# The down product of a feed-forward layer made by seven block products in place of eight

## The reference, cut to what matters

```python
def memory_cross_attention(h, mem_n, w_q, w_kv, w_o):
    q = (h @ w_q).reshape(B, T, XATTN_HEADS, XATTN_HEAD_DIM)
    ...
    p = jax.nn.softmax(s, axis=-1).astype(h.dtype)
    o = jnp.einsum('bhtm,bmhd->bthd', p, v).reshape(B, T, D_MODEL)
    return o @ w_o

def conv_glu_ffn(h, w_up, conv_w, conv_b, w_down):
    u = causal_dwconv(h @ w_up, conv_w) + conv_b
    a, b = jnp.split(u, 2, axis=-1)
    return (jax.nn.silu(a) * b) @ w_down          # [1024, 2816] @ [2816, 1024]

h = h + rmsnorm(y, g[5])                          # y is the layer's output
```

## Time and profile before

| what | value |
|---|---|
| median of 3 runs | 2668.46 us (2666.83 to 2671.12) |
| the profiled execution | 2670.99 us |
| its span | 2669.2 us |
| PE busy | 2591.1 us, 97% |
| DVE, ACT, POOL busy | 1659.6, 844.0, 1131.9 us |
| mean granted clock of TensorE | 0.992 |
| chain that ended last | PE 89%, DVE 4%, POOL 2%, ACT 2% |
| the down product's line (L2266) | 9% of that chain |

### The profile page before, as it was taken

How to read it: one execution, slowest core, us unless ns; L and a number is a source line. 1 busy time by engine, 2 the same in 40 slices (tenths; PEclk the granted TensorE clock), 3 DMA queues, 4 the chain that set the end, 5 groups by cost and what they waited for, 6 DMA issues and landing times.

```text
span 2669.2 us, 33144 instructions
## 1 busy us (share of the span) xinstructions
PE 2591.1 (97%) x13218; PEld 2174.4 (81%) x13218; DVE 1659.6 (62%) x2194; ACT 844.0 (32%) x1332; POOL 1131.9 (42%) x651
## 2 busy tenths in 40 slices
PE   6999899989999999999999999999999999999998
PEld 5788788877788777888888887888888888888887
DVE  4879978766512587666674558804555556476566
ACT  4011233334223433333332436212222222343342
POOL 2433100046632548777754444673223322242364
PEclk9999999999999999999999999999999999999999
DMA  4122333235312412222245553573333342466682
GB/s 153 56 94 97 99 124 127 95 104 206 112 62 79 158 58 86 79 87 79 87 149 191 169 178 121 186 258 106 134 111 111 130 147 94 159 251 211 223 315 111
DMA packets 147381, 360.25 MB, mean 135 GB/s; under 512 B 15173, under 2 KB 51229, under 8 KB 147100
## 3 DMA queue, kind: packets, MB, share of 16 engines
q1 hardware_dynamic: 65072, 177.81, 19.9%
q10 hardware_dynamic: 82156, 180.33, 18.9%
HBM read 268.90 MB, written 89.19 MB: 134 GB/s over the span
## 4 chain that ended last, share of the span: by engine, by line
PE 89%; DVE 4%; POOL 2%; ACT 2%; issue 1%; DMA 1%; ACTq 0%; POOLq 0%; DVEq 0%
PE pp L296 32%; PE pp L2213 13%; PE pp L494 11%; PE pp L2266 9%; PE pp L278 9%; PE pp L2953 2%; PE pp L1272 2%; POOL w_lo L3653 1%; PE pp L1944 1%; PE pp L1983 1%; POOL w_hi L3651 1%; DMA w_raw<-in_weights 1%; PE pp L1558 1%; PE pp L1597 1%; PE pp L444 1%
## 5 line engine op out<-in xcount | busy, mean ns | idle before, releaser
L3651 POOL CAST w_hi<-w_raw 128x1024 fp32r<-128x1024 f32 x184 | 222.2, 1207 | 990.3 <-PE pp L296 659.5
L296 PE MATMUL pp<-w_hi,act_hi 128*128 128x512 f32 x1344 | 535.9, 399 | 12.7 <-POOL w_lo L3653 9.9
L296 PE MATMUL pp<-w_lo,act_hi 128*128 128x512 f32 x1344 | 524.5, 390 | 0.0
L296 PE MATMUL pp<-w_hi,act_lo 128*128 128x512 f32 x1344 | 524.5, 390 | 0.0
L3653 POOL TENSOR_TENSOR w_lo<-w_raw,w_hi 128x1024 fp32r<-128x1024 f32 x184 | 468.9, 2549 | 14.7
L296 PEld LDWEIGHTS pp<-w_hi,act_hi 128*128 128x128 f32 x1344 | 253.0, 188 | 67.9 <-POOL w_lo L3653 10.8
L296 PEld LDWEIGHTS pp<-w_hi,act_lo 128*128 128x128 f32 x1344 | 252.6, 188 | 53.5
L296 PEld LDWEIGHTS pp<-w_lo,act_hi 128*128 128x128 f32 x1344 | 253.2, 188 | 48.3
L494 PE MATMUL pp<-act_hi,w_hi 128*128 128x512 f32 x480 | 192.7, 402 | 10.6 <-DVE act_lo L849 6.5
L2184 POOL TENSOR_TENSOR w_lo<-w_raw,w_hi 128x1024 fp32r<-128x1024 f32 x52 | 132.5, 2550 | 164.7 <-ACT w_hi L2178 164.6
L494 PE MATMUL pp<-act_lo,w_hi 128*128 128x512 f32 x480 | 190.5, 397 | 0.0
(11 more groups left out here) (468 smaller groups left out, 5282.9 us busy)
## 6 DMA issues: line engine op xcount, KB each, us to landing
w_raw<-in_weights SPq DMA_DIRECT2D x314, 512.0 KB, 3.5
z_s<-hg_st ACTq DMA_DIRECT2D x52, 512.0 KB, 4.1
hid_s<-ffn_cb ACTq DMA_DIRECT2D x22, 512.0 KB, 2.6
ffn_graw<-hid_s ACTq DMA_DIRECT2D x44, 256.0 KB, 3.1
hg_qkb<-hT_s SPq DMA_DIRECT2D x16, 512.0 KB, 8.1
qkvT_s<-mixin_o ACTq DMA_DIRECT2D x12, 512.0 KB, 2.8
gdn_qkv<-qkvT_s ACTq DMA_DIRECT2D x8, 768.0 KB, 6.4
front_x<-in_x ACTq DMA_DIRECT2D x8, 512.0 KB, 5.0
```

The costliest lines, as they stand in the source:

```text
L296: last = pe.matmul(dst, a[:, k, t * P:(t + 1) * P], columns(w, j, k, 0, n), start=(k == 0 and a is high and w is w_hi), stop=(k == NK - 1 ...
L3651: pool.tensor_copy(hi, raw).then_inc(w_split, 1)
```

## The change

**The down product.** The hidden activation (tokens by 2816) and the weights (2816 by 1024) are cut in two by two blocks: hidden rows are taken in pairs (even rows and odd rows; 11 pairs, `FG`), tokens in halves, output columns in halves. Seven block products (`DOWN`) take the place of eight. Each has 11 steps, a step being one 128x512 piece of activation (or of a sum) by one 128x512 piece of weights (or of a sum), for four tiles: 4 x 3 = 12 matmuls of 512 columns. So there are 77 steps and 77 x 12 = 924 matmuls.

**Sums of weights** (T1 to T4, `DownSums`): 11 groups of four blocks are loaded (1 MB each, three buffers), four subtractions of 128x512 are made on each group in place, and the group is stored. Groups 0 to 5 are loaded and stored by ACT's queue in Queries and subtracted by DVE there; groups 6 to 10 are loaded and stored by SP and subtracted by POOL, in its list after the fourth half of w_o's first strip, which is while attention runs. `softmax_of` for tiles 0 and 1 moves from Attention to Queries on DVE, in between.

**Sums of activations** (S1 to S4, `hidden_sums`): DVE makes four of 128x512 for each pair of finished hidden rows, ACT's queue stores them (1 MB), one pair in each two rounds of the up part, the first before `tlow(3)`.

**Weights of the down product.** From the third half on, SP loads the raw half to the place of its own low part, once PE has released that place; before, it went to `w_raw`. ACT makes the high part, DVE (POOL before) makes the low part in place (`split_half`). A half is two pieces, so two steps; the sixth half of each product is one piece.

**Pieces** have six buffers for the raw ones and five for the parts.

**Putting together.** ACT copies product 0 and 1 out (`keep`), DVE adds the others (`join` u, v, e, f, g, four additions of 128x512 each). Norms of tiles 0 to 3 stand at fixed steps (`FIRSTS`, `KEEPS`, `SECONDS`, `TURNS`, `HIGHS`). In HgInputs tiles 4 to 7 are turned after j = 1, 3, 4 and 5, PE waits for `join` g before j = 0 and 1, and ACT's list is reordered.

```diff
-FCHUNKS = ((0, 1, 2, 3), (4, 5, 6, 7))
-N_DOWN = len(FCHUNKS) * FG
+DOWN = (("A11", "B11"), ("A12", "B21"), ("S2", "T2"), ("S1", "T1"), ("S4", "B22"), ("S3", "T3"), ("A22", "T4"))
+DOWN_HALVES = (FG + 1) // 2
+N_DOWN = len(DOWN) * DOWN_HALVES // 2
...
+            def make(self, eng, S, k, n):
+                b11, b12, b21, b22 = (self.bufs[k % 3][:, i, :] for i in range(4))
+                eng.wait_ge(self.loaded[k % 3], self.loaded_before + 16 * (k // 3 + 1))
+                S.done(eng.tensor_tensor(b11, b12, b11, ALU.subtract), "T1")
+                S.done(eng.tensor_tensor(b12, b22, b12, ALU.subtract), "T3")
+                after(eng, S, "T3", n)
+                S.done(eng.tensor_tensor(b22, b22, b11, ALU.subtract), "T2")
+                after(eng, S, "T2", n)
+                S.done(eng.tensor_tensor(b21, b21, b22, ALU.subtract), "T4")
...
+            LOADS = {4: (0,), 5: (1,), 6: (2,), 10: (3,), 11: (4,), 12: (5,)}
+            STORES = {7: 0, 8: 1, 9: 2, 13: 3, 14: 4, 15: 5}
...
+            def dve(self, dve):
+                W, S = self.sums, self.next
+                for k in range(4):
+                    W.make(dve, W.by_dve, k, k)
+                S.softmax_of(dve, 0)
+                W.make(dve, W.by_dve, 4, 4)
+                S.softmax_of(dve, 1)
+                W.make(dve, W.by_dve, 5, 5)
...
-            def split_down(self, pool, j):
-                for i in range(2):
-                    r, q = RAW_AT[j] + i, PART_AT[j] + i
-                    after(pool, self.down_cast, "cast", 2 * (j - FIRST_STRIP["down"]) + i)
-                    pool.tensor_tensor(w_lo[SLOT[q]][:, :], w_raw[:, r % 2 * HALF:(r % 2 + 1) * HALF], w_hi[SLOT[q]][:, :].bitcast(F32), ALU.subtract).then_inc(w_ready, 1)
...
+                eng.tensor_tensor(w_lo[SLOT[q]][:, 0:n], self.raw_half(m), w_hi[SLOT[q]][:, 0:n].bitcast(F32), ALU.subtract).then_inc(w_ready, 1)
...
+                    for a, b in ((0, 0), (0, 1), (1, 0)):
+                        last = pe.matmul(self.down_bank(p, u), g[a][:, u * P:(u + 1) * P], w[b], start=(fresh and k == 0 and a == 0 and b == 0),
+                                         stop=(k == FG - 1 and a == 1), skip_group_check=True)
...
+                    elif p == 1:
+                        after(pe, self.kept, f"s{u}", 0)
...
+                    elif p == 3:
+                        after(pe, J, f"u{u}", 0)
...
+            FIRSTS = {56: 0, 58: 1, 60: 2, 69: 3}
+            KEEPS = {58: 0, 60: 1, 62: 2, 71: 3}
+            SECONDS = {62: 0, 67: 1, 71: 2, 74: 3}
+            TURNS = {64: 0, 69: 1, 73: 2}
+            HIGHS = {66: 0, 70: 1, 74: 2}
...
+                for n in range(self.STEPS):
+                    p, k = n // FG, n % FG
                     high(n + 2)
-                    cast_down(n + 3)
-                    load(n + 4)
+                    if k % 2 == 0:
+                        cast_down(p * DOWN_HALVES + k // 2 + 3)
+                    load(n + 6)
...
+                    elif n == 10:
+                        keep(0, "s")
+                        store_sums(FG - 1)
...
+                hidden_sums(0, "S1", "S2")
                 tlow(3)
...
+                joins = {2: "u", 3: "v", 4: "e", 5: "f"}
+                for n in range(self.STEPS):
+                    p, k = n // FG, n % FG
+                    m = p * DOWN_HALVES + k // 2 + 2
+                    if n + 2 < self.STEPS:
                         low(n + 2)
+                    if k % 2 == 0 and m < 2 * N_DOWN:
+                        self.split_half(dve, m)
...
-                    for t in {1: (4,), 2: (5,), 3: (6, 7)}.get(j, ()):
+                    for t in {1: (4,), 3: (5,), 4: (6,), 5: (7,)}.get(j, ()):
...
+                if r == RAW_AT[FIRST_STRIP["o"]] + 6:
+                    xq.sums.by_sync(sp)
+                if 2 <= down < 2 * N_DOWN:
+                    sp.wait_ge(w_used, USED_BEFORE[ffn.place_of(down)])
...
+                    if j == FIRST_STRIP["o"] + 1 and i == 0:
+                        xq.sums.pool(pool)
```

More of the change, by code:

```diff
@@ L677, in act, with taps @@
                         self.next.exps_of(act, self.EXPS[j])
-        def taps(dve, V, name, rnd, dst, src, w, n, bias=None, amid=None):
-            for j in range(n):
+                    if j in W.STORES:
+                        W.store(act, W.STORES[j])
+                    if j == NT // 2 + 2:
+                        after(act, R.N, "xn", NT - 1)
+                    for k in W.LOADS.get(j, ()):
+                        W.load(act, k)
+            def dve(self, dve):
[6 more added lines that the diff above has]
+                W.make(dve, W.by_dve, 5, 5)
+        def taps(dve, V, name, rnd, dst, src, w, n, bias=None, amid=None, only=None):
+            for j in range(n) if only is None else (only,):
                 k = n - 1 - j
@@ L1998, in act, with softmax_of @@
                     A.done(act.activation(act_hi[:, :, t * P:(t + 1) * P], pp[2][:, :].rearrange("p (m n) -> p m n", m=NK), ACT.Copy), "hi")
+            def softmax_of(self, dve, t):
+                V = self.dves
+                if t == 0:
+                    V.start(dve)
+                st, p = self.st[:, t % 2], self.p[t % 2]
+                after(dve, self.scored, "s", t)
+                if t >= 2:
+                    after(dve, V, "p3", t - 2)
+                if t < 2:
+                    for i in range(2):
+                        two = bank((1, 3, 5, 7)[2 * t + i]).rearrange("p (h m) -> p h m", h=2)
+                        V.done(dve.tensor_reduce(st[:, 0, 2 * i:2 * i + 2], two, AX_X, ALU.max), ("max0", "max")[i])
+                else:
+                    V.done(dve.tensor_reduce(st[:, 0, :], pp[3 * (t % 2)][:, :].rearrange("p (h m) -> p h m", h=XH), AX_X, ALU.max), "max0", "max")
+                after(dve, V, "max", t)
+                V.done(dve.tensor_scalar(st[:, 1, :], st[:, 0, :], -XD ** -0.5, None, ALU.mult), "neg")
+                after(dve, self.exps, "e3", t)
+                V.done(dve.reciprocal(st[:, 3, :], st[:, 2, :]), "r")
+                after(dve, V, "r", t)
+                for h in range(XH):
+                    V.done(dve.tensor_scalar(p[:, h, :], p[:, h, :], st[:, 3, h:h + 1], None, ALU.mult), f"p{h}")
@@ L2089, in __init__ @@
                 self.down_cast = carried_on(mixin.an, "cast", 1)
-                self.kept = carried_on(delta.fa, "kept", 4)
+                self.kept = carried_on(delta.fa, " ".join(f"{n}{u}" for n in "sc" for u in range(NT // 2)), 4)
                 self.ghs = sem_steps("ffn_ghs", "hi")
@@ L2097, in __init__ @@
                 self.loaded = sem("ffn_loaded")
+                self.raw_lo = [at(f"raw_lo{s}", [P, HALF], lo_at + 4 * HALF * s) for s in range(4)]
                 self.hid_stored, self.stored_before = mixin.stored, 16 * 6
-                self.hid_loaded, self.loaded_before = front.loaded, 16 * NT // front.SLOTS
                 spare = {"at": spare_at}
@@ new lines, in place_of, with slot_loaded, raw_half @@
+            def place_of(self, m):
+                return PART_AT[FIRST_STRIP["down"] + m // 2] + m % 2
+            def slot_loaded(self, m):
+                W, s = self.weight_sums, m % 4
+                done, before = (W.loaded[s], W.loaded_before) if s < 3 else (W.stored[0], W.stored_before[0])
+                return done, before + 16 * (len(range(s % 3, FG, 3)) + m // 4 + s // 2)
+            def raw_half(self, m):
+                n, r = self.filled(m), RAW_AT[FIRST_STRIP["down"]] + m
+                if 2 <= m < 2 * N_DOWN:
+                    return self.raw_lo[SLOT[self.place_of(m)]][:, 0:n]
+                return w_raw[:, r % 2 * HALF:r % 2 * HALF + n]
@@ L2180, in split_down @@
[L2180 to L2184 removed]
+                self.down_cast.done(act.activation(w_hi[SLOT[q]][:, 0:n], self.raw_half(m), ACT.Copy), "cast")
@@ L2675, in act @@
                 sig(1)
-                R.high(act, 5)
-                R.second(act, 7)
                 self.prev.cast_down(act, N_DOWN * 2 + 4)
```

409 lines of the change are left out of this document (271 added, 138 removed).

## The result

The changed kernel takes **2678.2 us** (median of 20 runs, 2667.7 to 2687.7); the kernel before, on the same chips, 2667.5 (20 runs, 2665.0 to 2671.1). The ratio is 1.0036, 95% interval 1.0029 to 1.0042: slower, by 10.7 us between the medians. I had forecast 2658.4, faster, and a range to 2672. Its runs also lie three times as far apart as those of before (20.0 us to 6.2).

A forecast was written before the change was run, and what follows sets the result against it. PE's work and whatever makes PE wait were taken as the bound; -30.0 - 1.6 + 11 + 3 + 8 - 0.5 = -10.1 us from the median 2668.46 gave 2658.4 us, range 2641 to 2672.

The forecast's parts named there:

- Feeding a step of half the length: Down product: loads, splits and list order make PE wait, +11 us in sum, from +3 to +25.
- rival 3: Gains eaten without loss, 2666 to 2674 us: loads of 4.5 us and a third attention tile caught; chance 0.17.
- slack of 1.9 us: Down product: piece ready 6.3 us after a step begins, wanted at 8.2, so the steady part costs nothing.
- the first hand-over: Down product, product 0 to 1: PE waits 3.0 us for ACT's copy, with slow clock 4.7 together.
- copying product 1 out: Down product: ACT's four copies of about 0.5 us use up the slack, costing 0.2 us.
- join u: Down product: DVE's low part and weights' part precede its additions; 0.5 us each for u and v, 1.2 with signals.
- Rival 4: Slower: down loads into the place PE just released make PE slip, over 2673.8 us from about 5.7 per load; chance 0.13.
- Matmuls -30.0: Down product: 924 matmuls in place of 1056, 132 fewer at 0.2273 us each, saves 30.0 us.
- The old wait -1.6: Down product: the one wait of 1.58 us that interrupted PE goes, saving 1.6 us.
- The up part +3: Up part: the first set of activation sums before `tlow(3)` pushes T3, T4 and c22 on DVE, +3 us.
- Attention +8: Attention: DVE's scalings wait for POOL's subtractions of weight sums, +8 us with slow clock, from 0 to 12.
- The tail -0.5: Behind the down product: -3 for tile 7's old wait, +2.5 for late weights of j = 2; -0.5 us (-3 to +3).

The follow-up runs named there:

- a_via_w_raw: Changed kernel with the raw halves of the down weights loaded through w_raw again, two in turn; 2658.4 us, ratio 0.9962 to the kernel before.
- j_raw_dve: a_via_w_raw with the first two halves after the down product split by DVE, not POOL; 2653.5 us, ratio 0.9947 to the kernel before.
- m_contiguous: Changed kernel with both sources of the down loads laid out so each load is one unbroken DRAM stretch; 2676.7 us, ratio 1.0036 to the kernel before.
- f_raw_orders: a_via_w_raw with ACT's copying out of products 0 and 1 and DVE's joins u, v, f reordered; 2664.3 us, ratio 0.9980 to the kernel before.

## Why the prediction was wrong, point by point

**What failed** is the step "Feeding a step of half the length", with its sentence "I take the 3.4 of the same queue and size". The price taken from the kernel before was 4.3 to 4.7 in the changed one. That was inside my upper bound, but rival 3 was the place where I had put 4.5 us, at +6 us on the items. It cost far more, for three reasons that the runs show:

- The slack of 1.9 us was reckoned with every load at its median. Loads spread from 3.4 to 8.8 us, and the first four long waits each have one of 6.0 to 8.8 in their chain, the one at 1498.16 nothing else. Not every long load stops PE: one of 5.7 us, issued at 1404.0, did not. The spread could be read beforehand, for the kernel before has it too, in the loads of w_raw from 1380 to 1595 us, where a feed that was ahead absorbed it:

```profile
DMA to landing us min/median/max: 3.3/3.4/9.6
```

- I charged the low clock once, to the first hand-over. It came after five of the six waits of about 3 us: 8.1 us in place of 1.7.
- Small items became long waits, since they came on top of a feed already late: copying product 1 out, which I had as 0.2, stands ahead of the wait of 3.11 us at 1443.85, and join u, which I had as 0.5 and signals, of the 2.95 at 1473.15. With the slack back (a_via_w_raw) PE has no wait over 0.5 us from the stage's start to 1550.

Rival 4 is the mechanism that took place, the wait for a place just released. I had it decide from 5.7 us per load. With a_via_w_raw's 21.9 us (248.4 - 226.5, or 19.7 by the medians) as its whole price, it decided at a median load of 4.7. I gave it 0.13.

A second failure is a term that the sum doesn't have at all: the 4.8 us at the start of the wide product. I had walked the places of the ring inside the down product only, and not what two halves fewer do to the stages behind it.

**The terms.** Matmuls -30.0: right in count and price (213.2 for 924 and the transposes closes the sum above). The old wait -1.6: not gone but replaced, ahead of the last transposes of the stage, by the 2.87 us at 1612.20. Feeding +11: +35.2 (248.4 - 213.2), 13.3 of it with the load off the path (226.5 - 213.2). That this is near 11 is luck in part, for it isn't made up as walked: in a_via_w_raw PE waits 0.17 us at the first hand-over, where I had 3.0 "fixed by order", nothing at joins u and v, 2.89 and 1.79 among the norms and the later joins, and 3.64 for POOL's splits, which the sum didn't have (without them, in j_raw_dve, 7.7 us are left of the 13.3). The up part +3: +2.7, 2.3 of it up to the first round's T4, which has 0.95 where it had 0.43 in the earlier trace rows:

```profile
1019.90 0.50 PE L2347 MATMUL pp<-ffn_T4hi,w_hi 128*128 128x512 f32 x1 [0.95 <-DVE ffn_T4lo L2717]
```

The other 1.8 is slow clock in this trace (granted 0.66 from 1003.31 to 1007.31), which the kernel before had at 961 instead. a_via_w_raw had it at 961 as well, and there PE waits 1.52 us for T3's low part, as walked.

Attention +8: **+2.0**. The mechanism is right: four scalings of 128x256 take 3.61 us beside POOL against 1.14, which no row of before could show. The Trainium skill (SBUF — State Buffer, "Who interferes with whom") has `tensor_scalar` among the forms that can take the port pair shared with GpSimd; this trace agrees, with that number, for the scaling by a per-partition value. The size was off since POOL's five sets didn't run without a break: it waited 2.4, 5.3 and 4.0 us for loads of 1 MB that land in 6.7 to 9.3, and touched two tiles, one of them in part. Without this miss the forecast would have been 6 us further off: luck. The tail -0.5: -1.7, within what I gave it. The casts for j = 2 came late as forecast (POOL 15.94 us idle before 1625.74, PE waits 1.21), and I had not followed the same list to j = 4 (PE waits 2.46); but the kernel before had 2.9 us of waits there too, with a granted clock of 0.50 from 1645.34 to 1649.34, where the changed kernel has 1.00 behind both of its waits.

**What I had not walked**: POOL's two splits for the next product beside DVE's last low parts. The prediction had POOL leave the stage and forgot that it comes back before the end. It cost a_via_w_raw 5.6 us by the stage's length in j. In the changed kernel it stands ahead of the wait of 2.87 at 1612.20; no run took it away there while the feed stayed as it is.

**What stays open**: why the load lengthened (the traffic during the load is the theory left), and how much of it is the queue and how much the memory. The Trainium skill (DMA: Bandwidth & Descriptors, "Latency and other measured facts") gives the memory's access latency as 0.2 us on average and 2 us at high load. A lengthening of 0.9 to 1.3 us would fit into that difference of 1.8 us, an estimate from the page's two figures; no run here shows that the memory is the cause.

## What to carry to other kernels

Where a change lets a transfer start only when the busiest engine lets go of its place, count the lead from that release, with the slow end of the transfers' spread and with the traffic of the new kernel; what the releaser column says before ("waits for PE": the feed is ahead) is the very thing that the change may turn round. Loading straight into the released place took that lead away here: the same seven products with their raw halves in a buffer of their own, and with POOL kept out of DVE's way at the end, run at 0.9947 (0.9939 with longer rows) of the kernel before. A wait of about 3 us of PE's brought a slow clock in five of six cases, at 1.3 to 2.0 us each: a likely cost, not a certain one. And where a change alters how many places of a ring a stage takes, look at the stages behind it as well: here two halves fewer go with 4.8 us lost some 185 us later.

## What the runs showed of the hardware

- Behind a wait of some 3 us, PE's next 4 us ran at a mean granted clock of 0.50 to 0.68 in five of six cases of the changed kernel's down product, and at 1.00 in the remaining one (3.17 us, 1569.19). In a_via_w_raw a wait of 2.89 us (1550.28) was followed by 1.00 too.
- Two `tensor_tensor` of DVE on 128x512, 0.69 us each, took 5.29 us together beside POOL's two splits of 128x1024 (5.15), about as long as those.
- A load of 512 KB took 3.9 to 4.9 us at the median of a stage, whether its source lay in rows of 2 KB, rows of 4 KB or in one stretch; with 256 KB more in front of each it took 5.1 to 5.6, and 3.4 in the kernel before. Within one stage such loads spread from 3.3 to 9.6 us (before).
- The executions of the changed kernel spread over 20 us (20 runs), those of the kernel before over 5 to 9 us (9 to 22 runs). That the feed makes the difference isn't shown: m_contiguous, fed as the changed kernel is, spread over 5.7 us (5 runs), and f_raw_orders, with the slack back, over 13.5 (11 runs).
